# Half-width scaling and copies in the gated scan, and two query tiles ahead of the key transposition

## What is computed

```python
def gla_scan(q, k, v, g):                     # gated linear attention, 4 heads
    b = cumsum(g)                              # of log forget gates, inside a chunk
    attn[t, s] = sum_d q[t,d] * k[s,d] * exp(b[t,d] - b[s,d])    # s <= t
    o = (q * exp(b)) @ state + attn @ v
    state = exp(b_last) * state + (k * exp(b_last - b)).T @ v

o_b = rms_norm(o_b, gla_norm_g) * silu(g_r)    # "yb" in the kernel
dq, dk, dv = ...                               # projections of the sparse attention
score = sum_h relu(iq_h . ik) * iw_h ; top 128 keys of each query ; softmax over them
```

## Time and profile before

| | |
|---|---|
| median of 3 runs | 1885.24 us (1879.75 to 1888.14) |
| the profiled execution | 1880.21 us, of which 1878.3 us span |
| PE busy | 1671.3 us, 89% |
| POOL busy | 1012.1 us, 54% |
| DVE busy | 930.4 us, 50% |
| ACT busy | 496.5 us, 26% |
| granted PE clock, mean | 0.94 |

### The profile page before, as it was taken

How to read it: one execution, slowest core, us unless ns; L and a number is a source line. 1 busy time by engine, 2 the same in 40 slices (tenths; PEclk the granted TensorE clock), 3 DMA queues, 4 the chain that set the end, 5 groups by cost and what they waited for, 6 DMA issues and landing times. The chain is left out here.

```text
span 1878.3 us, 20749 instructions
## 1 busy us (share of the span) xinstructions
PE 1671.3 (89%) x7778; PEld 1311.7 (70%) x7778; DVE 930.4 (50%) x1437; ACT 496.5 (26%) x939; POOL 1012.1 (54%) x945
## 2 busy tenths in 40 slices
PE   4999798998979979999998699999897699999995
PEld 2778576776757757778876487666574578888884
DVE  7784654498773361231315861865457433133134
ACT  2201322313241121124444422433444420010011
POOL 2767553455717435757870345222374167777772
PEclk8999899998999978999999799998898799999997
DMA  9355211133212032314545532101121013223211
GB/s 362 141 199 197 98 67 68 56 112 113 90 68 90 1 135 93 143 68 157 191 152 187 212 101 90 45 24 45 46 90 68 23 68 105 97 90 112 91 68 45
DMA packets 32694, 197.54 MB, mean 105 GB/s; under 512 B 3735, under 2 KB 7591, under 8 KB 10964
## 3 DMA queue, kind: packets, MB, share of 16 engines
q1 hardware_dynamic: 26040, 179.57, 26.2%
q10 hardware_dynamic: 5836, 14.03, 2.2%
q0 software_dynamic: 720, 2.62, 0.4%
HBM read 190.90 MB, written 7.66 MB: 106 GB/s over the span
## 5 line engine op out<-in xcount | busy, mean ns | idle before, releaser
L2488 POOL TENSOR_TENSOR b_wlo<-b_raw,b_whi 128x512 fp32r<-128x512 f32 x516 | 705.5, 1375 | 70.5 <-ACT b_whi L1507 35.4
L2482 POOL TENSOR_SCALAR b_whi<-b_raw 128x512 fp32r<-128x512 f32 x420 | 312.1, 743 | 760.0 <-PE ps L436 578.2
L434 PE MATMUL ps<-b_hhi,b_whi 128*128 128x512 f32 (+1 forms) x1112 | 450.1, 405 | 27.4 <-POOL b_wlo L2488 8.0
L435 PE MATMUL ps<-b_hlo,b_whi 128*128 128x512 f32 (+1 forms) x1112 | 439.5, 395 | 0.0
L436 PE MATMUL ps<-b_hhi,b_wlo 128*128 128x512 f32 (+1 forms) x1112 | 438.6, 394 | 0.0
L434 PEld LDWEIGHTS ps<-b_hhi,b_whi 128*128 128x128 f32 x1112 | 213.6, 192 | 91.6 <-issue 45.0
L436 PEld LDWEIGHTS ps<-b_hhi,b_wlo 128*128 128x128 f32 x1112 | 213.5, 192 | 45.6
L435 PEld LDWEIGHTS ps<-b_hlo,b_whi 128*128 128x128 f32 x1112 | 213.9, 192 | 44.5 <-issue 2.4
L434 PE MATMUL ps<-b_ahi,b_whi 128*128 128x512 f32 x432 | 176.4, 408 | 12.5 <-DVE b_alo L1721 6.2
L435 PE MATMUL ps<-b_alo,b_whi 128*128 128x512 f32 x432 | 171.6, 397 | 0.0
L436 PE MATMUL ps<-b_ahi,b_wlo 128*128 128x512 f32 x432 | 171.2, 396 | 0.0
(11 more groups left out here) (335 smaller groups left out, 2118.8 us busy)
## 6 DMA issues: line engine op xcount, KB each, us to landing
b_raw<-in_stream SPq DMA_DIRECT2D x165, 1024.0 KB, 4.8
bias_near<-bias_vectors ACTq DMA_DIRECT2D x1, 2298.0 KB
b_x<-in_xT SPq DMA_DIRECT2D x1, 2048.0 KB, 13.1
b_x<-in_xT ACTq DMA_DIRECT2D x1, 2048.0 KB, 7.7
h_tokens<-b_y ACTq DMA_DIRECT2D x1, 2048.0 KB, 11.8
b_arena<-in_cw ACTq DMA_DIRECT2D x1, 2048.0 KB, 7.3
out<-b_x SPq DMA_DIRECT2D x8, 256.0 KB, 2.0
bias_compressed<-bias_vectors ACTq DMA_DIRECT2D x1, 1024.0 KB
```

The source lines that it names most:

```text
L434: pe.matmul(o, ahi_, bhi_, start=start, stop=False)
L435: pe.matmul(o, ahi_, blo_, start=False, stop=False)
L2482: nc.gpsimd.tensor_scalar(whi[:, s, c], raw[:, r, c], 1.0, 1.0, ALU.mult, ALU.mult)\
L2488: nc.gpsimd.tensor_tensor(wlo[:, s, c], raw[:, r, c], whi[:, s, c].bitcast(F32), ALU.subtract)\
```

## The change

Two parts.

On DVE: at levels 0 to 6 the two multiplications cover only the halves that the level joins: of `qs` the upper half of each block, of `ksc` the lower half, so 512 columns each instead of 1024. At levels 2 to 6 the predicated copies cover only the upper halves: 256 columns instead of 512. What the matmuls make of the columns that are not scaled anew is not copied, as before.

On PE and ACT: `dq` 0, 1 stand ahead of the key transposition and use banks 6 and 7; the turn of the banks 0 to 5 then starts anew. `dq` 2, 3 follow the outputs `og`, then `sum_og` of heads 0, 1, `index_products(1)`, and `sum_og` of heads 2, 3. ACT squares heads 2 and 3 ahead of the reciprocal root of head 0.

```diff
--- before.py
+++ after.py
@@ -653,6 +653,9 @@
             linear("gr", range(2, 4), KD, hhi, hlo, 0, "gla_r")
             level(6)
             level(7)
+            share_banks(main=[6, 7])
+            linear("dq", range(2), KD, hhi, hlo, 0, "dq_read")
+            share_banks(main=[0, 1, 2, 3, 4, 5])
             pe.wait_ge(sem("khat"), 1)
             for c in range(ST - 1):
                 o = open_bank(("khat", c), "ktok")
@@ -690,11 +693,12 @@
                     mark(pe.matmul(o[:, 0:(T + 1) * P], iq[r, h // 2, T * P:(T + 1) * P], ik[r, 0:(T + 1) * P],
                                    start=True, stop=True), ("idx", T, h))
 
-            for a in range(2):
-                linear("dq", range(2 * a, 2 * a + 2), KD, hhi, hlo, 0, "dq_read")
-                for h in (2 * a, 2 * a + 1):
-                    norm_sum(("sum_og", h), 1)
+            linear("dq", range(2, 4), KD, hhi, hlo, 0, "dq_read")
+            for h in range(2):
+                norm_sum(("sum_og", h), 1)
             index_products(1)
+            for h in range(2, 4):
+                norm_sum(("sum_og", h), 1)
             linear("dk", range(2), KD, hhi, hlo, 0, "dk_read")
             index_products(2)
             linear("dk", range(2, 4), KD, hhi, hlo, 0, "dk_read")
@@ -1350,11 +1354,13 @@
             for h in range(4):
                 evacuate(("og", h), og[:, h, :], "og_read")
             finished(act, ("og", 3))
+            act.wait_ge(sem("og_read"), 4)
+            squares_of(2, lambda k: og[:, k, :])
             for a in range(2):
-                act.wait_ge(sem("og_read"), 4)
-                squares_of(2, lambda k: og[:, 2 * a + k, :])
                 for m in (2 * a, 2 * a + 1):
                     evacuate(("dq", m), dq[:, m, :], "dq_read")
+                if a == 0:
+                    squares_of(2, lambda k: og[:, 2 + k, :])
                 for h in (2 * a, 2 * a + 1):
                     rstd_of(("sum_og", h), P, slot=h % 2)
                     hi_of("yb", h, ahi[:, 4 + h, :])
@@ -1874,14 +1880,20 @@
             def flat(t):
                 return t.rearrange("p a t -> p (a t)")
 
+            def halves(t, lv, upper):
+                b_ = 1 << lv
+                return t.rearrange("p (n b) -> p n b", b=2 * b_)[:, :, upper * b_:upper * b_ + b_]
+
             for lv in range(LEVELS):
                 if lv < LEVELS - 1:
                     dve.wait_ge(sem("decay"), lv + 1)
                     dve.wait_ge(sem("decay_lower"), lv + 1)
                     if lv:
                         finished(dve, ("level", lv - 1, ST - 1))
-                    run(V.tensor_tensor(flat(qs), flat(qg), edec, ALU.mult), "level_scaled", False)
-                    run(V.tensor_tensor(flat(ksc), flat(kg), edec, ALU.mult), "level_scaled")
+                    run(V.tensor_tensor(halves(flat(qs), lv, 1), halves(flat(qg), lv, 1), halves(edec, lv, 1), ALU.mult),
+                        "level_scaled", False)
+                    run(V.tensor_tensor(halves(flat(ksc), lv, 0), halves(flat(kg), lv, 0), halves(edec, lv, 0), ALU.mult),
+                        "level_scaled")
                 if lv < LEVELS - 2:
                     difference(lv + 1)
                 if lv == LEVELS - 1:
@@ -1892,10 +1904,16 @@
                                         ALU.subtract), "decay_diff")
                 for n in range(4):
                     finished(dve, ("level", lv, n))
-                    mask = levelmask[:, lv, :].bitcast(U32).unsqueeze(1).to_broadcast([P, 4, P])
                     at_ = (n % 2) * 1024 + (n // 2) * 512
-                    run(V.copy_predicated(attn[:, at_:at_ + 512].rearrange("p (h t) -> p h t", h=4), mask,
-                                          tiles(bank(("level", lv, n)), 4)), "level_read")
+                    dst, new, mask = attn[:, at_:at_ + 512], bank(("level", lv, n)), levelmask[:, lv, :].bitcast(U32)
+                    if 2 <= lv < LEVELS - 1:
+                        nb = P >> (lv + 1)
+                        mask = halves(mask, lv, 1).unsqueeze(1).to_broadcast([P, 4, nb, 1 << lv])
+                        dst, new = (halves(t, lv, 1).rearrange("p (h n) b -> p h n b", h=4) for t in (dst, new))
+                    else:
+                        mask = mask.unsqueeze(1).to_broadcast([P, 4, P])
+                        dst, new = tiles(dst, 4), tiles(new, 4)
+                    run(V.copy_predicated(dst, mask, new), "level_read")
                 if lv in (0, 3):
                     ups(0, range(4) if lv == 0 else range(4, 8))
             dve.wait_ge(sem("decay"), LEVELS + 1)
```

## The result

The changed kernel takes 1895.49 us (median of 17 runs, 1883.65 to 1900.46), the kernel before 1884.64 (17 runs, 1879.75 to 1888.8). The ratio is 1.0056, with a 95% interval of 1.0042 to 1.007: 10.9 us slower. The forecast was 1892, and the time lies in its range of 1880 to 1901. By its own bound of 0.5% the time is just on the slower side, which had 0.28 against 0.65 for "within"; the interval, from 0.42% to 0.7%, reaches across that bound.

A forecast was written before the change was run, and what follows sets the result against it. It took PE and DVE in turn as the bound, with DVE setting the pace from yb on. Bank waits +11.2 and levels -4.0 gave +7.2, from the median 1885.2 to 1892 us; range 1880 to 1901.

The forecast's parts named there:

- The path: PE and DVE through the levels, PE to yb, DVE to mod_sum(11)'s end; each microsecond index(2) starts later delays the end equally.
- one sign of being wrong: The prediction called itself wrong if, among other signs, mod_sum(11)'s start moved by less than index(2)'s.
- The filled wait: PE's 7.48 us wait before the key transposition: dq 0, 1 fill it, with the first output product at 324.2.
- The waits for banks, +11.2: From yb to index(2): PE waits for dq and index banks, so index(2) starts 11.2 us later, bounds +8 and +13.
- The levels, -4.0: Levels 0, 1, 4: shorter multiplications save 2.6 us of PE's waits, the clock 1.4; together -4.0, bounds 0 and -9.3.
- halves cost what the whole did: Rival, chance 0.20: DVE walks over skipped columns, levels 0 and 1 gain nothing, level 4 gains 0.8; 1896 us.
- the 1.4 us that I added for the clock: At levels 1 and 4, a shorter wait no longer lets PE's clock fall: 1.4 us gained, range 0 to 3.2.
- The low rival: "The banks don't bind", chance 0.12: dk 0, 1 run beside yb as before, index(1) comes 2 us earlier; 1879 us.
- the 2 us that the forecast takes for POOL's absence: From root 2 to index(1): POOL has nothing to split there, so 8.3 us instead of 10.3.

The follow-up runs named there:

- the fourth experiment: The third experiment's kernel with the sums of heads 0, 1 put between dq 2 and dq 3: 1872.84 us, ratio 0.9949 to the kernel before.
- the ninth: The fourth experiment's kernel with square and root buffers per head, each sum behind the next head's output product, banks handed out anew: 1859.4 us, ratio 0.9872.
- the fifth experiment: The changed kernel with ACT's squares of heads 2, 3 back behind the high part of head 1: 1894.23 us, ratio 1.0053.
- the first experiment: The kernel before with only the halves in the levels' multiplications and copies, order and banks as before: 1883.53 us, ratio 1.0001.
- the tenth: The ninth experiment's kernel with whole-tile scaling and copies in the levels: 1864.9 us, ratio 0.9892.
- the third experiment: The changed kernel with other banks, sums of heads 2, 3 right after heads 0, 1, first index products behind dk 0, 1: 1881.18 us, ratio 0.9979.

## Why the prediction came right, point by point

**The path.** Right. What index(2) lost arrived at the modulation product (20.1 and 19.8) and in the span (19.5); the fourth experiment moved yb forward and got it back at the end; in the ninth the wait that closes DVE's chain all but vanished. By the letter, one sign of being wrong came up: mod_sum(11) moved by less than index(2). It was 19.9 (445.76 for 425.83) against 20.1, too little to speak against the path.

**The filled wait.** Right: no wait in front of the transposition (320.18, no bracket), the first output product at 323.91 for 324.2.

**The waits for banks, +11.2.** Right in place and in size. Like with like, index(2) moved by 11.1, and by 11.3 with the order alone (393.08 for 381.82), where the levels ended within 0.1 us of before. Piece by piece, forecast and measured in the changed kernel:

| step | forecast | measured |
|---|---|---|
| end of dq 2, 3 to root 0 | 2.5 | 2.45 (354.76 to 357.21) |
| root 0 to the evacuation of dq 2 | 9.4 | 8.24 (to 365.45) |
| root 0 to root 2 | 12.7 | 12.62 (to 369.83) |
| root 2 to index(1) | 8.3 | 7.91 (to 377.74) |
| index(1) to dk | 0.5 | 0.54 (to 378.28) |
| dk to index(2) | 13.8 | 14.66 (to 392.94) |
| PE's wait for a dq bank | about 10 | 8.82 |
| PE's wait at dk | 7 to 8 | 7.44 |
| DVE's gap ahead of index(2) | 8 to 10 | 11.46 |
| PE's wait at dv | 3 | 2.78 |

The evacuation came 1.2 us sooner after root 0 than told, and root 2 came 4.4 after it where I had 3.3: 0.64 to the index products, 1.63 to the sums and 2.11 to the root, with the clock at 0.50 from 366 to 370. The gap of DVE is outside its range, 11.46 for 8 to 10: DVE had finished index(1) after 3.7 us (377.74 to 381.48) where the earlier trace rows have 5.1 to index(2), since POOL was not splitting beside it (busy for none of the 7.5 us from 374, and for 4.7 of the 9 us from 364 before), and index(2)'s products came 0.9 later. The 8.8 us of the output products are in none of these steps. I had set a changed kernel at full clock there beside the earlier trace rows, which are at full clock too, so in the difference the stretch cancels, as it does when both are at half. That the clock could be at half in one and not in the other the prediction had not considered, and by it the first pair of profiles differed by 8.6 us more than the medians.

**The levels, -4.0.** This is the term that the changed kernel's profile doesn't bear out, and the runs leave its size open. The waits came as told, 3.24 for the forecast 3.4, together 3.2 us less for the forecast 2.6 (timelines of PE, DVE and POOL, for the earlier trace rows):

```profile
203.67 5.13 PE L644 MATMUL ps<-b_arena 64*128 64x128 f32 x32 [8.59 <-DVE b_arena L1895]
...
225.16 3.86 PE L644 MATMUL ps<-b_arena 64*128 64x128 f32 x32 [3.24 <-DVE b_arena L1895]
...
222.75 0.69 DVE L1893 TENSOR_TENSOR b_arena<-b_arena 128x512 f32<-128x512 f32 x1
223.36 1.75 DVE L1895 TENSOR_TENSOR b_arena<-b_arena 128x512 f32<-128x512 f32 x1
...
222.79 1.77 POOL L2506 TENSOR_TENSOR b_wlo<-b_raw,b_whi 128x512 fp32r<-128x512 f32 x1
```

Two halves and POOL's subtraction in turn take 2.4 us (222.75 to 225.11), forecast 2.65, before 3.42. That a stepped 512-column multiplication takes 0.69, as a plain one, decides against the rival "halves cost what the whole did" at level 1; in the fifth experiment's profile the first of level 0, over every second column, takes 0.69 as well. The Trainium skill, SBUF — State Buffer, section "SBUF: two separate sides", has whichever of the two starts first hold the shared port pair for its whole instruction; by that rule POOL's operation beside DVE should shorten by what DVE's turn shortens, and it does: 2.30 to 1.77, as DVE's goes from 1.23 to 0.69.

What failed in the profile is the 1.4 us that I added for the clock. I had taken that a shorter wait could only help. In the windows from 226 on the clock is low longer than before, and now while PE multiplies densely:

```profile
226.00:228.00 2.00, 2.00 (x24) 2.00 (x23) 1.93 (x3) 1.29 (x3) 2.00 (x2) 0.67 0.03 8
228.00:230.00 2.00, 2.00 (x9) 1.58 (x8) 1.77 (x4) 1.14 (x1) 1.92 (x3) 0.50 0.00 0
230.00:232.00 2.00, 2.00 (x6) 1.61 (x5) 2.00 (x2) 0.00 (x0) 1.92 (x2) 0.50 0.00 0
232.00:234.00 2.00, 2.00 (x7) 1.52 (x7) 1.78 (x2) 0.00 (x0) 0.00 (x1) 0.63 0.57 82
```

In the profile of before the same four windows have 0.94, 0.50, 0.71 and 1.00. Level 1 starts 2.2 us sooner than in the earlier trace rows (225.16 for 227.38), level 2 only 0.6 sooner, and the levels end 0.2 sooner (309.17 for 309.34). How much the clock takes back differs from profile to profile. From the start of the wait in front of level 0 to the end of level 7, the four profiles with whole levels have 113.4 to 117.5 us (mean 114.7), the nine with halves 107.5 to 114.2 (mean 112.2). So the halves are worth about 2.5 us on the mean, with a spread larger than that. The runs don't settle it. With the halves the ratio is 0.0001 higher than without in the first experiment, whose interval ends at 3.4 us less; it is 0.002 lower in the changed kernel than with the order alone, and 0.002 lower in the ninth than in the tenth. 0.002 is 3.8 us, and in both pairs the intervals overlap. So the first experiment speaks against 4.0, the two pairs speak for nearly that, and what the halves are worth stays open between nothing and 4.

**The sum.** +11.2 - 4.0 = +7.2 was forecast, 10.9 measured (7.9 to 13.2 by the interval). If the banks cost 11.2, the missing 3.7 lie in the levels; if the levels brought their 2.5, some 2 us of it are the banks' or the clock's, and no run separates these. The rival "halves cost what the whole did" had nearly the right number (1896) for a wrong reason: the halves are as cheap as their columns.

**The low rival.** The 2 us that "the banks don't bind" takes off index(1) don't follow from the terms beside them: 3.9 later less 3.3 is 0.6 later. Only with the 2 us that the forecast takes for POOL's absence does it become 1.4 earlier, and with the levels 1880. In the third experiment index(2) came 1.4 earlier than in the second profile of before (380.47 for 381.82).

**The chances.** 0.28 for "slower by over 0.5%" came true at 0.56%, with an interval that reaches down to 0.42%, and 0.65 for "within" did not. With the levels' term between nothing and 2.5 us the forecast would have been 1894 to 1896, and the two chances about even.

## What to carry to other kernels

An instruction that is moved ahead on an in-order engine needs its bank as well as its inputs; follow the bank's last reader, since a PE wait that is filled at one place can come back as a wait for a bank that hangs on a chain of two other engines. Ask first which engine's chain sets the end: here filling 7.5 us of PE's idle time brought no more than 3.8 us even without the waits for banks (medians of the third experiment, halves included), and the root of a norm that came 4.6 us earlier was worth at least that. And take a second profile of the same kernel before a difference of two single profiles is explained: where the clock falls is part of the execution, and one stretch at half clock was 8 of the 19.5 us that the two spans differed by.

## What the runs showed of the hardware that I had not expected

- The granted clock can stay at 0.50 while PE is busy without a gap. In the output products of the changed kernel (128 x 128 fp32 matmuls) it was 0.50 from 328 to 344 with PE busy 8.00 of 8.00 us in both windows, after a wait of 1.3 us ahead of them; a head took 4.8 us instead of 2.7. In the ten profiles without dq 1 between the state updates and these products the clock fell there in eight (not in the first of before, and not in the ninth experiment's), in the three with it in none.
- A shorter wait need not shorten the stretch at low clock. Level 1's wait went from 4.30 to 3.24, and the clock was back at 1.00 in the window from 234 instead of the one from 232. From the start of level 1 to that of level 2, the same matmuls, three of the four profiles with the long wait have 15.4 to 15.5 us and one 17.0; of the nine with the short wait two have 15.4, five 17.0 and two 18.0 to 18.1.
- DVE's copies under a mask take less time for fewer columns, also where these are every second run of 4 to 64: 443 ns for 256 and 739 for 512 (groups of one line by form, the levels of the changed kernel). No wait of PE hangs on these copies, so all of that gain was off the path.

```profile
L1916 DVE COPY_PREDICATED b_arena<-b_con,ps 128x512 f32<-128x512 uint32 x12 | 8.9, 739 | 1.3 <-PE ps L644 1.0
L1916 DVE COPY_PREDICATED b_arena<-b_con,ps 128x256 f32<-128x256 uint32 x20 | 8.9, 443 | 38.8 <-PE ps L644 37.7
```
